# Splitting a head pair's value product by part: all high parts in the even head's step, all low parts in the odd head's

## The chip, the cores and the metric

The kernel runs on one core of a Trainium2 chip. The metric is the time of one execution on the device in microseconds (us). Engines are called PE (TensorE; PEld is its weight load), DVE (VectorE), ACT (ScalarE), POOL (GpSimd) and SP (SyncE). A wait is written "consumer <- producer".

## The reference

One layer of a hybrid backbone: an input projection, retention heads and attention heads side by side, an output projection, expert-choice experts and a final norm, for 2048 latent tokens and 128 context tokens. The change touches attention only, which for each block of 128 queries and each of 8 heads of width 64 computes

```
s = einsum('bkgqd,bskd->bkgqs', qblk, k) * scale     # 16 key tiles of latents and one of context
p = softmax(s, axis=-1)
o = einsum('bkgqs,bskd->bkgqd', p, v)
```

Latent queries read 17 key tiles (2176 keys), context queries only the context tile.

## The kernel before

Every fp32 product is made of high and low parts held as fp32r: a high part is a rounded copy (ACT), a low part what is left of the value (DVE subtracts). The stages follow one another with a barrier between them: conditioning, projection, retention, attention, output projection, selection, experts, final norm.

Attention goes over query tiles i = 0 to 15 (latent) and NT = 16 (context), and in each over heads h = 0 to 7. One pass for one head is called a step here. Tiles 2 to 14 are one loop body, the others are written out. Each engine has its own order of a step's events, a list written by hand: PE_STEP (L999), ACT_STEP (L1001), DVE_STEP (L1003). PE's is: turn 0, turn 1, value 0, value 1, turn 2, turn 3, scores 0, value 2, scores 2, turn 4, fold (even steps; modulation in steps 5 and 7), scores 1.

- `turn` n (L1264): transposes four key tiles of the head's probabilities (turn 4: one) into one of two PSUM banks `a_ps_t`, used alternately. It waits until the bank was emptied. ACT copies the bank into `a_pT_hi` (L1405), DVE subtracts that into `a_pT_lo` (L1507) and so empties the bank.
- `scores` n (L1246): scores of head h+2 for banks 0 and 1 (scores 0), 2 and 3 (scores 1) or 4 (scores 2). It waits until ACT's exponential has read the old scores (`exped`). DVE takes the maxima (L1480), which for scores 1 are the last and lead to the negated maximum `a_nm` (L1490).
- `value` (L1273): the values of a head pair (group) against its turned probabilities, summed in `a_ps_o`. The pair 2g, 2g+1 is taken in steps 2g+2 and 2g+3, in six pieces (PIECES, L1006), three in the even step and three in the odd one. For each key tile the high and the low matmul stand behind one another. The stationary operand is the values' tile (both parts side by side, 128 columns), the moving one the pair's 256 columns. Before the first piece PE waits for both banks to be emptied (the low parts of the step before) and for `o_kept` (ACT has copied the sums of the group before).
- `fold` (L1294) adds the halves of a finished group; DVE's `combine` (L1547) divides by the softmax sum. After step 3 the attention output of the tile before is turned (`out`, L1313), before step 6 the next tile's queries (`q`, L1234).

The context tile has only turn 4 and scores 2 in a step, but the first two of its steps still take the value pieces of tile 15's last pair; its own pairs are one key tile wide.

Of the kernel before, what the change touches and what calls it, by code (L numbers as in the profile page):

```python
# [15 lines left out]
NQ = 8  # L16
NKV = 2
QPK = NQ // NKV
# [973 lines left out]
KEY_TILES = NT + 1  # L992
# [3 lines left out]
CTX_KEYS = NT + 1  # L996
# [6 lines left out]
DVE_STEP = [("turn", 0), ("turn", 1), ("total", 0), ("turn", 2), ("turn", 3), ("scores", 0), ("turn", 4), ("scores", 2),  # L1003
            ("fold", 0), ("scores", 1)]
SEG_ORDER = [0, 2, 1]
PIECES = [(0, 3), (3, 6), (6, 9), (9, 12), (12, 15), (15, KEY_TILES)]  # L1006
GROUP = 2
NGRP = NQ // GROUP

# [1 line left out]
def attention(nc, g, a, s):  # L1011


    with ExitStack() as ctx:
# [4 lines left out]
        vals = k.sb("a_vals", [P, NK, NKV, 2, HD], F32R)  # L1019
# [7 lines left out]
        pT_hi = [k.sb(f"a_pT_hi{i}", [P, KEY_TILES, GROUP, P], F32R) for i in range(2)]  # L1027
        pT_lo = [k.sb(f"a_pT_lo{i}", [P, KEY_TILES, GROUP, P], F32R) for i in range(2)]
# [11 lines left out]
        ps_o = k.ps("a_ps_o", [P, GROUP, P])  # L1040
# [6 lines left out]
        sum_ok, rsum_ok, hi_kept = k.sem("a_sum_ok"), k.sem("a_rsum_ok"), k.sem("a_hi_kept")  # L1047
        filled, emptied = k.sems("a_filled", 2), k.sems("a_emptied", 2)
        fold_ok, valued, o_kept = k.sem("a_fold_ok"), k.sem("a_valued"), k.sem("a_o_kept")
# [95 lines left out]
        def group_index(i, n):  # L1145

            return i * NGRP + n
# [67 lines left out]
        def _(pe):  # L1215
# [57 lines left out]
            def value(t, grp, piece, uses_before):  # L1273

                ctx_tile = isinstance(t, int) and t == NT
                if piece == 0:
                    for b in range(2):
                        pe.wait_ge(emptied[b], uses_before[b])
                    if not (isinstance(t, int) and t == 0 and grp == 0):
                        pe.wait_ge(o_kept, group_index(t, grp))  # L1280
                lo, hi = PIECES[piece]
                kts = range(lo, hi) if not ctx_tile else ([KEY_TILES - 1] if piece == 0 else [])
                for c in kts:
                    src = CTX_KEYS if ctx_tile else c
                    for part in (pT_hi, pT_lo):
                        first = piece == 0 and c == kts[0] and part is pT_hi
                        last = part is pT_lo and c == KEY_TILES - 1
                        ins = nc.tensor.matmul(ps_o[:, :, :],  # L1288
                                               vals[:, src, grp * GROUP // QPK, :, :].rearrange("p d f -> p (d f)"),
                                               part[grp % 2][:, c, :, :], start=first, stop=last)  # L1290
                if kts and kts[-1] == KEY_TILES - 1:
                    ins.then_inc(valued, 1)

            def fold_halves(t, grp, bank):  # L1294
# [30 lines left out]
            start = Bank(-1)  # L1325
# [6 lines left out]
            def body(i):  # L1332
                bank = Bank(i)
                for h in range(NQ):
                    uses_before = [bank.uses_of(b) for b in range(2)]
                    for kind, n in step_events(i, h):
                        if kind == "q":
                            turn_queries(i + 1, n, bank)
                            q_uses = [bank.uses_of(b) for b in range(2)]
                        elif kind == "scores":  # L1340
                            scores(*score_of(i, h), n, q_uses if h >= NQ - 2 else None)
                        elif kind == "turn":
                            turn(i, h, n, bank)
                        elif kind == "value":
                            value(*group_of(i, h), h % 2 * 3 + n, uses_before)
                        elif kind == "fold":
                            fold_halves(*fold_of(i, h), bank)
                        elif kind == "mod":
                            modulation(i, n, bank)
                        else:  # L1350
                            turn_out(i - 1, n, bank)
                if isinstance(i, int) and i == NT:
                    uses_before = [bank.uses_of(b) for b in range(2)]
                    fold_halves(i, NGRP - 2, bank)
                    value(i, NGRP - 1, 0, uses_before)
                    fold_halves(i, NGRP - 1, bank)
                    for half_at in range(2):
                        turn_out(i, half_at, bank)
# [1248 lines left out]
```

## Time and profile before

| | |
|---|---|
| median of 3 runs | 3443.71 us (3442.35 to 3448.79) |
| profiled execution | 3446.82 us, of which the profile's span is 3445.1 us |
| PE busy | 3122.0 us (91%), PEld 2855.8 us (83%) |
| DVE, ACT, POOL busy | 1872.4 (54%), 1716.9 (50%), 396.7 us (12%) |
| mean granted TensorE clock | 0.951 |
| attention, 1000 to 1300 us: busy PE, DVE, ACT; clock | 291.15, 246.08, 224.46 us; 1.00 |
| first value matmul of a step to that of the next, steps 0 to 7, tile from 1205.61 us | 7.09, 6.38, 6.95, 7.58, 6.61, 9.83, 6.57, 7.43 us |
| waits of PEld's scores for ACT's exponential, 820 to 1600 us | 9.4 us, 27 times |
| value matmuls of attention (L1288) | 1092 with high and 1092 with low probabilities |

Where the table names no stretch it is over the whole span. Attention lies between about 690 and 1697 us, its steady part between 820 and 1655. In a timeline a row is a run of like instructions, with start, length, engine, line, operation, operands and count; in brackets stands the engine's idle time before it and what ended that. Matmuls are pipelined, so that the distance of starts, not the length of a row, is what one costs.

### The profile page before, as it was taken

To read this page: it belongs to the slowest core of one execution; us is meant where nothing else is said; L and a number is where in the kernel's file an instruction comes from. 1 tells how busy PE (TensorE), PEld (TensorE's weight loads), DVE (VectorE), ACT (ScalarE), POOL (GpSimd) and SP (SyncE) were. 2 spreads that over 40 slices of the span, in tenths; PEclk is the share of its full clock that TensorE was granted. 3 is DMA by queue.
4 is the path that set the end of the run, shared out by engine and by line. 5 is a ranking of instruction groups with operands and counts; after the bars stand their busy time and mean duration, and the time that the engine had idled before them with its cause. 6 is when DMAs were issued, how large, how long until landed. Compare 5 with 4: busy or idle time off the path is not lost. (4 is left out here: it accounts for less than half of the span.)

```text
span 3445.1 us, 59312 instructions
## 1 busy us (share of the span) xinstructions
PE 3122.0 (91%) x21600; PEld 2855.8 (83%) x21600; DVE 1872.4 (54%) x3255; ACT 1716.9 (50%) x3375; POOL 396.7 (12%) x386
## 2 busy tenths in 40 slices
PE   6899997769999999999699857999999999999991
PEld 6788886658888888888588756999999999999991
DVE  2122224858888888888533383554445555454543
ACT  2222222557777777777433334555554445554542
POOL 0233333500000000000000000111111111111101
PEclk9999998979999999999799857999999999999995
DMA  6112114311000000000244316666666566655546
GB/s 219 49 66 78 62 61 145 129 43 29 19 27 18 22 20 24 21 24 22 73 145 160 118 28 200 196 185 187 185 186 187 178 186 190 186 184 184 184 123 226
DMA packets 315924, 393.74 MB, mean 114 GB/s; under 512 B 30321, under 2 KB 272193, under 8 KB 314817
## 3 DMA queue, kind: packets, MB, share of 16 engines
q1 hardware_dynamic: 302000, 338.64, 30.1%
q0 software_dynamic: 10240, 35.66, 4.6%
q10 hardware_dynamic: 3600, 18.35, 1.3%
q8 instruction: 50, 0.82, 0.1%
q14 instruction: 34, 0.27, 0.0%
HBM read 318.68 MB, written 74.06 MB: 114 GB/s over the span
## 5 line engine op out<-in xcount | busy, mean ns | idle before, releaser
L2423 DVE TENSOR_TENSOR e_w_lo<-e_raw,e_w_hi 128x2048 fp32r<-128x2048 f32 x192 | 440.1, 2292 | 490.7 <-ACT e_w_hi L2365 490.7
L93 PE MATMUL e_ps<-e_x_hi,e_w_hi 128*128 128x272 f32 x2048 | 602.2, 294 | 5.5 <-issue 5.5
L95 PE MATMUL e_ps<-e_x_hi,e_w_lo 128*128 128x272 f32 x2048 | 593.9, 290 | 0.0
L94 PE MATMUL e_ps<-e_x_lo,e_w_hi 128*128 128x272 f32 x2048 | 590.3, 288 | 0.0
L1507 DVE TENSOR_TENSOR a_pT_lo<-a_ps_t,a_pT_hi 128x512 fp32r<-128x512 f32 (+1 forms) x648 | 368.3, 601 | 137.2 <-ACT a_pT_hi L1405 136.9
L1405 ACT ACTIVATE a_pT_hi<-a_ps_t 128x512 fp32r<-128x512 f32 (+1 forms) x648 | 319.6, 532 | 171.0 <-PE a_ps_t L1270 166.2
L93 PEld LDWEIGHTS e_ps<-e_x_hi,e_w_hi 128*128 128x128 f32 x2048 | 386.3, 189 | 7.1 <-issue 5.5
L94 PEld LDWEIGHTS e_ps<-e_x_lo,e_w_hi 128*128 128x128 f32 x2048 | 387.1, 189 | 0.0
L95 PEld LDWEIGHTS e_ps<-e_x_hi,e_w_lo 128*128 128x128 f32 x2048 | 386.1, 189 | 0.0
L2365 ACT ACTIVATE e_w_hi<-e_raw 128x2048 fp32r<-128x2048 f32 x192 | 366.1, 1907 | 14.6 <-DMA e_raw<-in_w_gate 10.2
L1480 DVE TENSOR_REDUCE a_mx<-a_ps_s 128x1 f32<-128x896 f32 (+2 forms) x392 | 346.7, 892 | 26.7 <-PE a_ps_s L1260 26.7
L1270 PE MATMUL a_ps_t<-ident,a_prob 128*128 128x128 f32 x2184 | 329.8, 280 | 27.3 <-DVE a_pT_lo L1507 17.1
L1260 PE MATMUL a_ps_s<-a_keys,a_qT 128*128 128x448 f32 (+2 forms) x1296 | 342.3, 379 | 8.6 <-ACT a_prob L1397 6.5
L1397 ACT ACTIVATE a_prob<-a_ps_s,a_nm 128x896 f32<-128x896 f32 (+2 forms) x392 | 334.9, 859 | 19.0 <-DVE a_nm L1490 16.6
L1270 PEld LDWEIGHTS a_ps_t<-ident,a_prob 128*128 128x128 f32 x2184 | 245.0, 141 | 81.1 <-DVE a_pT_lo L1507 49.0
L93 PE MATMUL e_ps<-e_h_hi,e_w_hi 128*128 128x272 f32 x1024 | 298.2, 291 | 0.0
L95 PE MATMUL e_ps<-e_h_hi,e_w_lo 128*128 128x272 f32 x1024 | 296.3, 289 | 0.0
L94 PE MATMUL e_ps<-e_h_lo,e_w_hi 128*128 128x272 f32 x1024 | 294.8, 288 | 0.0
L1288 PE MATMUL a_ps_o<-a_pT_hi,a_vals 128*128 128x256 f32 x1092 | 282.8, 292 | 2.6 <-DVE a_pT_lo L1507 1.5
L1288 PE MATMUL a_ps_o<-a_pT_lo,a_vals 128*128 128x256 f32 x1092 | 271.7, 282 | 0.0
L93 PE MATMUL p_psP<-w_in_hi,p_hhi 128*128 128x512 f32 (+1 forms) x680 | 254.3, 374 | 4.7 <-DVE p_hlo L415 4.7
L95 PE MATMUL p_psP<-w_in_hi,p_hlo 128*128 128x512 f32 (+1 forms) x680 | 255.6, 376 | 0.0
(284 smaller groups left out, 5430.7 us busy)
## 6 DMA issues: line engine op xcount, KB each, us to landing
e_raw<-in_w_gate SPq DMA_DIRECT2D x64, 1024.0 KB, 5.1
e_raw<-in_w_up SPq DMA_DIRECT2D x64, 1024.0 KB, 5.2
e_raw<-in_w_down SPq DMA_DIRECT2D x64, 1024.0 KB, 5.1
s_ret<-p_pr SPq DMA_DIRECT2D x17, 768.0 KB, 3.6
m_raw<-in_w_in ACTq DMA_DIRECT2D x8, 1152.0 KB, 7.7
o_cT<-s_ct SPq DMA_DIRECT2D x17, 512.0 KB, 5.0
s_x<-o_x SPq DMA_DIRECT2D x17, 512.0 KB, 5.0
s_xn<-o_xn SPq DMA_DIRECT2D x17, 512.0 KB, 3.7
```

What stands on the lines that cost most here:

```text
L93: nc.tensor.matmul(out, w_hi, x_hi, start=first, stop=False)
L94: nc.tensor.matmul(out, w_hi, x_lo, start=False, stop=False)
L95: return nc.tensor.matmul(out, w_lo, x_hi, start=False, stop=last)
L1260: ins = nc.tensor.matmul(ps_s[:, b, 0:w], qT[:, h, :], keys[:, part, h // QPK, src:src + w], start=(part == 0), stop=(part == 1))
L1270: ins = nc.tensor.transpose(ps_t[b][:, c % 4, :], prob[h % 2][:, c * P:(c + 1) * P], g["ident"][:, :])
L1288: ins = nc.tensor.matmul(ps_o[:, :, :], vals[:, src, grp * GROUP // QPK, :, :].rearrange("p d f -> p (d f)"), part[grp % 2][:, c, :, :], s ...
L1397: nc.scalar.activation(seg_probs(i, h, seg), seg_scores(seg, seg_width(i, seg)), ACT.Exp, bias=nm[:, h % 2:h % 2 + 1], scale=scale, accum_ ...
L1405: nc.scalar.activation(out, ps_t[b][:, 0:out.shape[1], :], ACT.Copy).then_inc(hi_kept, 1)
L1480: nc.vector.tensor_reduce(mx[:, h % 2, seg:seg + 1], seg_scores(seg, seg_width(i, seg)), AXY, ALU.max)\
L1507: nc.vector.tensor_tensor(pT_lo[h // 2 % 2][:, out, h % 2, :], ps_t[b][:, 0:m, :], pT_hi[h // 2 % 2][:, out, h % 2, :].bitcast(F32), ALU.s ...
L2365: nc.scalar.activation(w_hi[n % RING][:, :, :], raw[n % RING][:, :, :], ACT.Copy).then_inc(w_hi_ok, 1)
L2423: nc.vector.tensor_tensor(w_lo[n % RING][:, :, :], raw[n % RING][:, :, :], w_hi[n % RING][:, :, :].bitcast(F32), ALU.subtract).then_inc(w_ ...
```

## The change

The pieces become (0, 6), (6, 11), (11, 17), and the even step takes all of them with the high parts, the odd step all again with the low parts. The wait for the emptied banks moves from the even step's first piece to the odd step's; the even step's first piece waits for the pair's last high copy (`hi_kept`) instead. The context tile's own groups keep one high and one low matmul in piece 0 and both waits, and wait for the banks in the odd step too, ahead of an empty piece. The sum of `a_ps_o` is of the same products in another order.

```diff
-PIECES = [(0, 3), (3, 6), (6, 9), (9, 12), (12, 15), (15, KEY_TILES)]
+PIECES = [(0, 6), (6, 11), (11, KEY_TILES)]
@@ value(t, grp, piece, uses_before)
-                if piece == 0:
+                low, n = divmod(piece, len(PIECES))
+                if n == 0 and (low or ctx_tile):
                     for b in range(2):
                         pe.wait_ge(emptied[b], uses_before[b])
+                if piece == 0:
+                    if not ctx_tile:
+                        pe.wait_ge(hi_kept, (t * NQ + GROUP * (grp + 1)) * 5)
                     if not (isinstance(t, int) and t == 0 and grp == 0):
                         pe.wait_ge(o_kept, group_index(t, grp))
-                lo, hi = PIECES[piece]
-                kts = range(lo, hi) if not ctx_tile else ([KEY_TILES - 1] if piece == 0 else [])
-                for c in kts:
-                    src = CTX_KEYS if ctx_tile else c
-                    for part in (pT_hi, pT_lo):
-                        first = piece == 0 and c == kts[0] and part is pT_hi
-                        last = part is pT_lo and c == KEY_TILES - 1
-                        ins = nc.tensor.matmul(ps_o[:, :, :],
-                                               vals[:, src, grp * GROUP // QPK, :, :].rearrange("p d f -> p (d f)"),
-                                               part[grp % 2][:, c, :, :], start=first, stop=last)
-                if kts and kts[-1] == KEY_TILES - 1:
+
+                def product(c, src, part, first, last):
+                    return nc.tensor.matmul(ps_o[:, :, :], vals[:, src, grp * GROUP // QPK, :, :].rearrange("p d f -> p (d f)"),
+                                            part[grp % 2][:, c, :, :], start=bool(first), stop=bool(last))
+
+                if ctx_tile:
+                    if piece == 0:
+                        product(KEY_TILES - 1, CTX_KEYS, pT_hi, True, False)
+                        product(KEY_TILES - 1, CTX_KEYS, pT_lo, False, True).then_inc(valued, 1)
+                    return
+                for c in range(*PIECES[n]):
+                    ins = product(c, c, pT_lo if low else pT_hi, not low and c == 0, low and c == KEY_TILES - 1)
+                if piece == 2 * len(PIECES) - 1:
                     ins.then_inc(valued, 1)
```

## Rows read from the trace of the kernel before

**Rows 1.** Waits from 820 to 1600 us: total us, times, longest

```profile
PEld a_ps_t L1270 <- DVE a_pT_lo L1507: 38.2, 131, 0.7
```

**Rows 2.** Instructions on the tile a_ps_o: ns min/median/max; engine idle before them

```profile
L1288 PEld LDWEIGHTS a_ps_o<-a_pT_hi,a_vals x1092: 186/188/333, 753.9 to 1691.7; 128*128 128x128 f32 x182
...
  DVE a_pT_lo L1507: 3.4, 4
```

**Rows 3.** Timeline of PEld, end of step 7 to step 1: turns, first value loads

```profile
1204.62 1.00 PEld L1270 LDWEIGHTS a_ps_t<-ident,a_prob 128*128 128x128 f32 x8
1205.59 0.19 PEld L1288 LDWEIGHTS a_ps_o<-a_pT_hi,a_vals 128*128 128x128 f32 x1
...
1211.71 1.00 PEld L1270 LDWEIGHTS a_ps_t<-ident,a_prob 128*128 128x128 f32 x8
1212.68 0.19 PEld L1288 LDWEIGHTS a_ps_o<-a_pT_hi,a_vals 128*128 128x128 f32 x1
```

**Rows 4.** Timeline, step 0: three value matmuls in sequence

```profile
1206.77 0.28 PE L1288 MATMUL a_ps_o<-a_pT_lo,a_vals 128*128 128x256 f32 x1
...
1206.89 0.28 PE L1288 MATMUL a_ps_o<-a_pT_hi,a_vals 128*128 128x256 f32 x1
...
1207.01 0.28 PE L1288 MATMUL a_ps_o<-a_pT_lo,a_vals 128*128 128x256 f32 x1
```

**Rows 5.** Timeline, step 0: low parts of turns 0 and 1; turns 2, 3

```profile
1206.82 1.29 DVE L1507 TENSOR_TENSOR a_pT_lo<-a_ps_t,a_pT_hi 128x512 fp32r<-128x512 f32 x2 [0.33 <-ACT a_pT_hi L1405]
...
1207.57 0.42 PEld L1270 LDWEIGHTS a_ps_t<-ident,a_prob 128*128 128x128 f32 x4 [0.48 <-DVE a_pT_lo L1507]
...
1208.16 0.42 PEld L1270 LDWEIGHTS a_ps_t<-ident,a_prob 128*128 128x128 f32 x4 [0.17 <-DVE a_pT_lo L1507]
```

**Rows 6.** Timeline, steps 4 and 6: the same instructions

```profile
1234.08 1.29 DVE L1507 TENSOR_TENSOR a_pT_lo<-a_ps_t,a_pT_hi 128x512 fp32r<-128x512 f32 x2 [0.60 <-ACT a_pT_hi L1405]
...
1235.01 0.90 PEld L1270 LDWEIGHTS a_ps_t<-ident,a_prob 128*128 128x128 f32 x8
...
1250.47 1.29 DVE L1507 TENSOR_TENSOR a_pT_lo<-a_ps_t,a_pT_hi 128x512 fp32r<-128x512 f32 x2 [0.94 <-ACT a_pT_hi L1405]
...
1251.46 0.90 PEld L1270 LDWEIGHTS a_ps_t<-ident,a_prob 128*128 128x128 f32 x8
```

**Rows 7.** Timeline, steps 1 and 3: exponential, turn 4 and scores 1

```profile
1216.20 1.03 ACT L1397 ACTIVATE a_prob<-a_ps_s,a_nm 128x896 f32<-128x896 f32 x1
...
1217.02 0.27 PE L1270 MATMUL a_ps_t<-ident,a_prob 128*128 128x128 f32 x1
1217.37 1.08 PE L1260 MATMUL a_ps_s<-a_keys,a_qT 128*128 128x448 f32 x4
...
1230.38 0.27 PE L1270 MATMUL a_ps_t<-ident,a_prob 128*128 128x128 f32 x1
1230.65 1.08 PE L1260 MATMUL a_ps_s<-a_keys,a_qT 128*128 128x448 f32 x4
```

**Rows 8.** Timeline, steps 5 and 7: turn 4, modulation, and what follows

```profile
1245.15 0.27 PE L1270 MATMUL a_ps_t<-ident,a_prob 128*128 128x128 f32 x1
1245.26 1.85 PE L1309 MATMUL a_ps_t<-cc,a_wm 128*128 128x2 f32 x16
...
1248.50 1.09 ACT L1408 ACTIVATE a_qT<-a_ps_t 128x512 fp32r<-128x512 f32 x2 [2.76 <-PE a_ps_t L1241]
...
1261.08 0.27 PE L1270 MATMUL a_ps_t<-ident,a_prob 128*128 128x128 f32 x1
1261.35 1.06 PE L1309 MATMUL a_ps_t<-cc,a_wm 128*64 128x2 f32 x16
```

**Rows 9.** Timeline, context tile, steps 0 and 1

```profile
1670.29 0.36 PE L1288 MATMUL a_ps_o<-a_pT_hi,a_vals 128*128 128x256 f32 x1 [0.29 <-issue]
...
1674.12 0.28 DVE L1550 TENSOR_TENSOR a_att<-a_ps_t,a_rsum 128x128 f32<-128x128 f32 x1
...
1675.18 0.34 PE L1260 MATMUL a_ps_s<-a_keys,a_qT 128*128 128x128 f32 x2
```

## The prediction

> **What bounds the kernel now.** I first read the busy shares by slice of the page: in attention PE is busy nearly throughout, DVE and ACT well over half. The table by stretch says the same of 300 steady us (in the table above): PE 291 us, DVE 246, ACT 224, the clock at its full level, 1.00. So PE sets the time, unless it waits. The list of waits says for whom: 131 times in 780 us PE's next transposes wait for DVE's low parts, 38.2 us in all [rows 1], and 27 times, two in a tile, the scores wait for ACT's exponential (9.4 us). The timeline of one tile then shows where in a step. The tile between 1205 and 1264 us (58.4 us, the sum of the step lengths in the table above) stands for 16; its step lengths return in the tiles of the loop within 0.05 us.
>
> In a step the wait is at turns 2 and 3, behind pieces 0 and 1. Turn 2 needs the bank of turn 0, which DVE frees with its first low part, turn 3 that of turn 1. In step 0 the two low parts run from 1206.82 to 1208.11; turn 2 starts at 1207.57, turn 3 at 1208.16, each right behind its own [rows 5]. Steps 1, 2, 3, 5 and 7 look the same (a wait of about 0.18 us before turn 3 in each). The low parts in turn hang on scores 1 of the step before, over the last maxima. So in six steps of eight the time goes round a ring: scores 1, maxima, low parts, turn 3, and then PE's own work up to the next scores 1. Pieces 0 and 1 lie beside the ring. Piece 2 lies on it.
>
> **The waits that are moved.** The wait taken from the even step is empty before the change. Turns 0 and 1 stand ahead of it on PE and have waited for the same two banks. The trace agrees: DVE ends idle time before a value matmul 4 times in all, 3.4 us, mostly in the context tile [rows 2]. The waits' own price: from the first load of turns 0 and 1 to the first value load it is 0.97 us in step 0 (three waits) and 0.97 us in step 1 (none) [rows 3]. So one wait fewer in the even step and two more in the odd one are priced at 0. What is queued behind them on PE are the value matmuls; who waits for those is ACT's copy of the sums, a step later. Bounds: a gain of 3.4 us, and a loss of 0.01 us in each of 64 odd steps, under 1 us.
>
> **Order of the matmuls.** 34 matmuls per pair before and after. Neighbours start 0.12 us apart, from low to high (other weights) as from high to low (same weights) [rows 4]. So giving up the neighbours with equal weights costs 0. Every matmul has a load of its own even now; the 1092 high ones have 1092 loads [rows 2]. The Trainium skill, "TensorE: Matmul & The Clock Gate", section "Step-by-step: what each phase is for", speaks against the change here: weights should be loaded once and used by several matmuls. By this rule the old order would have saved a load per pair and the new one lose it; the trace does not agree, as both transitions take 0.12 us.
>
> **Where the matmuls go.** Pieces were 6, 6, 6 matmuls in the even and 6, 6, 4 in the odd step; they become 6, 5, 6 in both. So pieces 0 and 1 shrink from 12 to 11 everywhere, piece 2 stays 6 in even steps and grows from 4 to 6 in odd ones.
>
> Pieces 0 and 1: PE comes 0.12 us earlier to turn 2. In the six steps of the ring it waits that much longer: 0. In steps 4 and 6 PE is the later one. In step 4 the low parts end at 1234.08 + 1.29 = 1235.37; turn 2 loads from 1235.01, turn 3 four loads of some 0.11 us later, at 1235.46 [rows 6]. With 0.05 us from DVE's end to PE's start (1208.11 to 1208.16 in step 0, [rows 5]) turn 3 can't start before 1235.42, so 0.04 us is gained. In step 6: low parts until 1251.76, turn 3 at 1251.91 [rows 6], gain 0.10 us. Together 0.14 x 16 tiles = 2.2 us gained. Bounds: 0 and 0.24 x 16 = 3.8 us.
>
> Piece 2, odd steps: 2 x 0.12 = 0.24 us more between turn 3 and scores 1, by step:
> - Step 5: turn 4 at 1245.15, the modulation right behind at 1245.26, then scores 1 and the queries' transposes, for which ACT has waited 2.76 us [rows 8]. Nothing covers it: +0.24.
> - Step 1: scores 1 starts at 1217.37, 0.35 us after turn 4, where a transpose takes 0.11; it waits for the exponential that runs from 1216.20 to 1217.23 [rows 7], which itself hangs on turn 3. Cover 0.24 us, all of it used: 0. If that cover is gone, +0.24.
> - Step 3: scores 1 comes 0.27 us after turn 4 [rows 7], cover 0.16. Scores 1 is 0.08 late, but the transposes of the output behind it wait for DVE (turn 4's low part): 0. Without that, +0.08 to +0.24.
> - Step 7: the modulation comes 0.27 us after turn 4 [rows 8]; it waits for DVE's low part of turn 3. Cover 0.16 by the starts of the matmuls, and more if their loads can run ahead: +0.00 to +0.08, I take 0.04. In tile 15 turn 4 waits for DVE anyway: 0.
>
> Sum: 16 x 0.24 + 15 x 0.04 = 3.8 + 0.6 = 4.4 us lost. Bounds: 0, were there cover in step 5 too, and 64 x 0.24 = 15.4 us, were there none at all.
>
> **The context tile.** Step 0 takes 17 matmuls instead of 18 (0.12 us), and its first no longer waits for DVE's copy of the modulation; it had idled 0.29 us there [rows 9]. So 0.4 us early. Step 1 now waits, ahead of the low parts, for the banks of step 0, the last of which is freed by DVE's division, 1674.12 + 0.28 = 1674.40 [rows 9]; before, the 16 matmuls followed the fold at once. They start at 1674.0 (0.4 early), take 17 x 0.12 + 0.08 = 2.1, and scores 2 follows at 1676.1 to 1676.2 instead of 1675.18 [rows 9]: +1.0 us, on a chain of latencies, so all of it. In steps 3, 5 and 7 the empty piece waits for the banks too, with scores 2 (turn 4 in step 7) queued behind it; the scores there wait longer for ACT. 0, with a bound of 1 us for the three.
>
> **Sum.** -2.2 + 4.4 + 1.0 = +3.2 us, on the profiled execution's 3446.82 us (1.7 us outside its span): 3450.0. That execution is 3.1 us above the median of the three runs; on the median, 3443.71 + 3.2 = 3446.9 us.
>
> **The rivals.** (A) As summed, +1 to +6 us. Chance 0.62.
> (B) Neutral: PE's work is the same and what one piece loses the other gets back; step 5 has cover, or steps 4 and 6 give their full 0.24. -3 to +1 us, 3441 to 3445. For it: nothing is added. Against it: the ring [rows 5] and ACT's 2.76 us [rows 8]. Chance 0.14.
> (C) Faster: the lifted wait is real where the profile doesn't show it. That gives at most 3.4 us [rows 2], with the full 3.8 us in steps 4 and 6 and all of piece 2 covered: -7.2 us, 3436.5. The change doing nothing of what it says (the wait is met anyway) is part of A and B. Chance 0.06.
> (D) Slower: the ring takes all of piece 2's growth in every odd step, because the cover in steps 1, 3 and 7 moves along with the delay. 15.4 - 2.2 + 1.0 = +14.2 us, 3457.9. It decides from about half of that cover on. For it: the cover in step 1 is exactly used up. Against it: the exponential hangs on turn 3, which isn't moved. Chance 0.17.
> (E) Reloading weights costs after all: a load of 0.19 us against a spacing of 0.12 [rows 2, 4] leaves 0.07 us bare in some 1088 low matmuls, 76 us, 3520. The equal spacings say no. Chance 0.01.
>
> **How the numbers follow.** About 0.2% (6.9 us) is what a measurement of this kernel tells from no change. A and B lie within it: same 0.76. C is faster, 0.06. D and E are slower, 0.18. The range reaches from B and the lower part of the runs' own scatter, 3440, to D's 3458; C and E stay outside.
>
> **What would show it.** In the trace after: 17 matmuls in each step's pieces; turns 2 and 3 of steps 0, 1, 2, 3, 5, 7 behind DVE's low parts as before, with the wait 0.12 us longer; the time from step 5's first value matmul to step 6's up from 9.83 to 10.07 us, from step 1's to step 2's unchanged at 6.38; the wait for the exponential gone in step 1; the first low matmul of the context tile's step 1 behind DVE's division. It is wrong if the steps 1 and 3 grow, if steps 0 or 2 change, or if matmuls with changing weights stand more than 0.12 us apart.

## The result and the profile after

The changed kernel takes 3453.06 us in the median of 20 runs (3447.52 to 3455.16), the kernel before 3444.42 us (20 runs, 3441.68 to 3448.89). The ratio is 1.0023, with a 95% interval of 1.0017 to 1.0030: slower by 5.9 to 10.3 us. The forecast was +3.2 us. The time lies inside the stated range, but the likeliest case, A, was too small, and the outcome fell on the side that had been given 0.18. Ratios are taken over the undisturbed executions: among the 15 of the kernel before that stand beside e5 to e8, one took 10325.14 us at a granted clock of 0.294 and is left out.

Two lines of the page of the changed kernel, its span and the busy times of PE, PEld, DVE, ACT and POOL:

```profile
span 3449.9 us, 59378 instructions
PE 3119.0 (90%) x21600; PEld 2853.3 (83%) x21600; DVE 1872.6 (54%) x3255; ACT 1716.5 (50%) x3375; POOL 396.9 (12%) x386
```

The engines work no longer than before (PE 3122.0, DVE 1872.4, ACT 1716.9 us) and run the same number of matmuls. What was lost is waiting. Two rows of the waits from 820 to 1600 us (total us, times, longest):

```profile
PEld a_ps_t L1270 <- DVE a_pT_lo L1513: 51.4, 159, 0.9
PE a_ps_t L1270 <- DVE a_pT_lo L1513: 19.7, 51, 0.7
```

The wait of the transposes' weight loads for the low parts went from 38.2 us in 131 waits [rows 1] to 51.4 in 159, as had been expected of pieces 0 and 1, which are one matmul shorter. The 28 new waits, two in a tile, stand before turn 2 of steps 1 and 3, where the list had shown none. In the matmuls' own row it went from 12.9 us in 39 waits to 19.7 in 51. The wait of PE's scores for ACT's exponential (9.4 us, 27 times before) is no longer in the list.

The distances between the first value matmuls of neighbouring steps tell where the time went. A typical tile of the loop, in us; equal steps agree from tile to tile and from run to run within about 0.03 us. e6 and e9, left out here, have the step lengths of e2 and of the changed kernel. "12/6" means 12 value matmuls ahead of turn 2 and 6 behind turn 3:

| kernel | even, odd steps | 0 | 1 | 2 | 3 | 4 | 5 | 6 | 7 | tile |
|---|---|---|---|---|---|---|---|---|---|---|
| before | 12/6, 12/4 | 7.09 | 6.38 | 6.95 | 7.57 | 6.62 | 9.83 | 6.57 | 7.43 | 58.44 |
| after | 11/6, 11/6 | 7.08 | 6.37 | 6.96 | 7.57 | 6.61 | 10.05 | 6.56 | 7.63 | 58.83 |
| e1, old order | 11/6, 11/6 | 7.07 | 6.37 | 6.96 | 7.57 | 6.62 | 10.05 | 6.57 | 7.62 | 58.83 |
| e2 | 11/6, 13/4 | 7.07 | 6.38 | 6.96 | 7.57 | 6.61 | 9.83 | 6.56 | 7.44 | 58.42 |
| e3 | 13/4, 13/4 | 6.90 | 6.40 | 6.96 | 7.57 | 6.62 | 9.84 | 6.57 | 7.44 | 58.30 |
| e4 | 11/6, 9/8 | 7.07 | 6.51 | 6.88 | 7.69 | 6.62 | 10.31 | 6.56 | 7.86 | 59.50 |
| e5 | 9/8, 13/4 | 7.32 | 6.38 | 7.20 | 7.54 | 6.62 | 9.83 | 6.57 | 7.45 | 58.91 |
| e7, old order | 13/6, 13/2 | 7.09 | 6.38 | 6.96 | 7.57 | 6.62 | 9.85 | 6.57 | 7.44 | 58.48 |
| e8, old order | 13/4, 11/6 in steps 0, 1 | 6.89 | 6.41 | 6.96 | 7.57 | 6.62 | 9.83 | 6.57 | 7.44 | 58.29 |

After the change only steps 5 and 7 differ, by 0.22 and 0.19 to 0.20 us. From the first value matmul of attention to the modulation of tile 15's step 7 it is 915.06 us before (753.88 to 1668.94) and 921.16 after (754.74 to 1675.90): 6.1 us. From there to the last transposes of attention it is 25.74 us (to 1694.68) and 26.96 (to 1702.86): 1.2 us. So attention carries 7.3 us, inside the interval of the runs. The spans of the two profiled executions differ by 4.8 us only. Outside attention they scatter: the one after begins attention 0.9 us later and makes up 3.4 us behind it, in stages that the change doesn't touch.

Step 5 after the change, answering to [rows 8]:

```profile
1249.48 0.27 PE L1270 MATMUL a_ps_t<-ident,a_prob 128*128 128x128 f32 x1
1249.58 1.85 PE L1315 MATMUL a_ps_t<-cc,a_wm 128*128 128x2 f32 x16
1251.29 1.05 PE L1260 MATMUL a_ps_s<-a_keys,a_qT 128*128 128x448 f32 x4
```

The modulation again starts 0.10 us behind turn 4: nothing lies between, and everything after it is late by the two matmuls. Step 7, with the low parts of turns 2 and 3:

```profile
1264.22 1.29 DVE L1513 TENSOR_TENSOR a_pT_lo<-a_ps_t,a_pT_hi 128x512 fp32r<-128x512 f32 x2 [0.77 <-ACT a_pT_hi L1411]
...
1265.62 0.27 PE L1270 MATMUL a_ps_t<-ident,a_prob 128*128 128x128 f32 x1
...
1265.82 1.09 PE L1315 MATMUL a_ps_t<-cc,a_wm 128*64 128x2 f32 x16
```

Here turn 4 and modulation are 0.20 us apart, although the low part of turn 3 had ended at 1265.51. Before they were 0.27 apart [rows 8]. So the cover had been at most 0.07 us, not 0.16. From turn 4 to scores 1 it is 1.27 us before (1261.08 to 1262.35) and 1.22 after (1265.62 to 1266.84), which leaves 0.24 - 0.05 = 0.19 us of growth, as measured.

### The profile page after: what moved, and what is told of

It reads as the page before. It is cut to its first block and busy times, and to the rows that moved or that the text cites. A ratio compares the mean times of both kernels' runs of the same rounds, so it can differ in the third digit from the quotient of the medians.

```text
span 3449.9 us, 59378 instructions
## 1 busy us (share of the span) xinstructions
PE 3119.0 (90%) x21600; PEld 2853.3 (83%) x21600; DVE 1872.6 (54%) x3255; ACT 1716.5 (50%) x3375; POOL 396.9 (12%) x386
## 5 line engine op out<-in xcount | busy, mean ns | idle before, releaser
L2371 ACT ACTIVATE e_w_hi<-e_raw 128x2048 fp32r<-128x2048 f32 x192 | 366.1, 1907 | 14.7 <-DMA e_raw<-in_w_gate 10.3
L94 PE MATMUL p_psP<-w_in_lo,p_hhi 128*128 128x512 f32 (+1 forms) x680 | 253.8, 373 | 0.0
L1260 PEld LDWEIGHTS a_ps_s<-a_keys,a_qT 128*128 128x128 f32 x1296 | 219.1, 192 | 20.2 <-ACT a_prob L1403 5.3
```

What stands on the lines that cost most here:

```text
L94: nc.tensor.matmul(out, w_hi, x_lo, start=False, stop=False)
L1260: ins = nc.tensor.matmul(ps_s[:, b, 0:w], qT[:, h, :], keys[:, part, h // QPK, src:src + w], start=(part == 0), stop=(part == 1))
L2371: nc.scalar.activation(w_hi[n % RING][:, :, :], raw[n % RING][:, :, :], ACT.Copy).then_inc(w_hi_ok, 1)
```

## Experiments

**e1: the new sizes in the old order.** The kernel before, with only this (and the loop over single matmuls that it needs):

```diff
-PIECES = [(0, 3), (3, 6), (6, 9), (9, 12), (12, 15), (15, KEY_TILES)]
+PIECES = [(0, 6), (6, 11), (11, 17), (17, 23), (23, 28), (28, 2 * KEY_TILES)]
...
+                for m in range(lo, hi):
+                    c, part = m // 2, (pT_hi, pT_lo)[m % 2]
```

> The old order (high and low matmul of a key tile behind one another) and the old waits, but the pieces hold 6, 5, 6 matmuls in both steps, as in the changed kernel. Theory R (the sizes alone: two more matmuls in the odd step's piece 2, which stands between turn 3 and scores 1): step 5 at 10.05 us and step 7 at 7.63 us as in the changed kernel, the other steps as before, the context tile as before; about +6 us on the time before, ratio 1.0015 to 1.002. Rival O (the new order of the matmuls or the moved waits cost the time): steps 5 and 7 at 9.83 and 7.44 us, ratio 1.000.

Measured: 3452.68 us against 3445.58, ratio 1.0020 (1.0011 to 1.0029), and the step lengths are those of the changed kernel, within 0.02 us. High beside low with equal weights, or 17 high ones in a row with changing weights, with the waits in the old or the new place: no step tells them apart. Rival O fell, and the title of the change describes the part of it that costs nothing. That the context tile stayed as before could not be read off here, since the clock was low in part of it:

```profile
1676.32:1679.61 3.29, 3.29 (x17) 3.29 (x18) 0.15 (x1) 0.00 (x0) 0.00 (x0) 0.59 0.02 5
```

This is the stretch view (time, then busy PE, PEld, DVE, ACT, POOL, granted clock, DMA share, GB/s) of the first value matmuls of that tile; the clock averages 0.59. Behind it the loss of the changed kernel is absent: from the fold to the last transposes of attention it is 22.04 us in e1 (1680.16 to 1702.20), 21.85 before (1672.83 to 1694.68) and 23.52 after the change (1679.34 to 1702.86).

**e2: the odd step's piece 2 back at 4.** The changed kernel with

```diff
+LOW_PIECES = [(0, 7), (7, 13), (13, KEY_TILES)]
-                for c in range(*PIECES[n]):
+                for c in range(*(LOW_PIECES if low else PIECES)[n]):
```

> The changed kernel with the low pieces cut 7, 6, 4 instead of 6, 5, 6, so that the odd step's piece 2 has its old 4 matmuls and pieces 0 and 1 together 13; the high pieces stay 6, 5, 6. Theory R: steps 5 and 7 back at 9.83 and 7.44 us, steps 1 and 3 unchanged (turn 2 comes up to 0.1 us later there, turn 3 had waited 0.18 us), so only the context tile's 1.2 us are left: ratio 1.000 to 1.0005. Rival O: nothing comes back, ratio 1.002. Rival S (PE's work in a step counts, wherever it stands): as the odd step still has 17 matmuls instead of 16 and the even one 17 instead of 18, the ratio of the changed kernel stays.

Measured: 3445.61 us against 3445.58, ratio 1.0001 (0.9992 to 1.0010). Steps 5 and 7 are back at 9.83 and 7.44 us with the order, the waits and the 17 matmuls per step of the changed kernel. So it is neither the order nor the amount of work in a step (rival S), but what stands behind turn 3 in the odd steps.

**e4: the odd step's piece 2 at 8.** Low pieces (0, 5), (5, 9), (9, KEY_TILES).

> The changed kernel with the low pieces cut 5, 4, 8: two more matmuls behind turn 3 in odd steps than in the changed kernel. Theory R: the cover by ACT's exponential in steps 1 and 3 (0.24 and 0.16 us) was used up by the first two, so now all four odd steps of a tile grow by 0.24 us over the changed kernel: 0.96 us per tile, 15 us in all, ratio to the time before 1.006 to 1.0075. If steps 1 and 3 have cover beyond that: ratio about 1.0045. Rival O: ratio 1.002.

Measured: 3462.29 us against 3445.58, ratio 1.0046 (1.0032 to 1.0060): the second of the three cases. Steps 5 and 7 grow by 0.26 and 0.23 us over the changed kernel, again the whole of two matmuls. Step 1 grows by 0.14 and step 3 by 0.12, and step 2 gets 0.08 back. The cover in steps 1 and 3 was larger than read. Turn 4 and scores 1 of these two steps in e4:

```profile
1227.21 0.27 PE L1271 MATMUL a_ps_t<-ident,a_prob 128*128 128x128 f32 x1
1227.23 1.06 PE L1261 MATMUL a_ps_s<-a_keys,a_qT 128*128 128x448 f32 x4
...
1240.62 0.27 PE L1271 MATMUL a_ps_t<-ident,a_prob 128*128 128x128 f32 x1
1240.65 1.05 PE L1261 MATMUL a_ps_s<-a_keys,a_qT 128*128 128x448 f32 x4
```

With nothing to wait for, scores 1 starts 0.02 and 0.03 us behind turn 4, not 0.11. Before the change it was 0.35 and 0.27 [rows 7], so the cover was 0.33 and 0.24 us. In step 1 that leaves 0.48 - 0.33 = 0.15 of four matmuls, as measured. In step 3 half of the remaining 0.24 was taken elsewhere; the prediction named the output's transposes, which no run isolates.

**e3: 13 and 4 everywhere.** PIECES = [(0, 7), (7, 13), (13, KEY_TILES)] for both parts.

> The changed kernel with all pieces cut 7, 6, 4: 13 matmuls ahead of turn 2 and 4 behind turn 3 in both steps. Theory R: even steps have 2 matmuls fewer on the ring. Steps 0 and 2 lose 0.24 us each, for turns 2 and 3 had waited longer there than the one added matmul takes; steps 4 and 6 between 0 and 0.24 us each, as they are held by ACT's chain or by PE; odd steps as before the change. Per tile -0.5 to -0.95 us, in all -7 to -14 us on the time before with the context tile's +1.2: ratio 0.996 to 0.998. Rivals O and S: ratio 1.000 to 1.002, since the same matmuls stand in the same order as in the changed kernel.

Measured: 3446.31 us against 3445.58, ratio 1.0001 (0.9992 to 1.0010). A miss of theory R. Two matmuls fewer behind turn 3 brought 0.17 us in step 0 and nothing in steps 2, 4 and 6. The ring alone doesn't tell the length of an even step; something else is level with it. That led to theory C, tested from both sides by e5 and e7.

**e5: the even step's piece 2 at 8.** High pieces (0, 5), (5, 9), (9, KEY_TILES), low pieces as in e2.

> High pieces 5, 4, 8, low pieces 7, 6, 4: the even step has 9 matmuls ahead of turn 2 and 8 behind turn 3, the odd step 13 and 4. Taking two away from the even step's piece 2 had changed nothing in steps 2, 4 and 6 and 0.17 us in step 0. Theory C (two chains run from turn 3 to scores 1 side by side: PE's own work, and ACT's copy and DVE's low part of turn 3, for whose bank the fold waits; with 6 matmuls in piece 2 they are nearly level): two matmuls more lie bare but for a small remainder, steps 0, 2, 4 and 6 grow by 0.15 to 0.24 us each, 0.6 to 0.9 us per tile. Rival X (steps 2, 4 and 6 are held by ACT's or DVE's work altogether, PE has room): they stay at 6.96, 6.62 and 6.57 us, only step 0 grows.

Measured (one execution, 3449.93 us): against e2, steps 0 and 2 grow by 0.25 and 0.24 us, steps 4 and 6 stay at 6.62 and 6.57. Theory C held in steps 0 and 2 and rival X in steps 4 and 6, which keep their length whether 4, 6 or 8 matmuls stand behind turn 3 (with 13, 11 or 9 ahead of turn 2). ACT's timeline of step 6, in the changed kernel, shows why:

```profile
1252.81 1.09 ACT L1414 ACTIVATE a_qT<-a_ps_t 128x512 fp32r<-128x512 f32 x2 [2.75 <-PE a_ps_t L1241]
1253.78 0.39 ACT L1423 ACTIVATE a_o_sum<-a_ps_o 128x256 f32<-128x256 f32 x1
1254.15 1.09 ACT L1411 ACTIVATE a_pT_hi<-a_ps_t 128x512 fp32r<-128x512 f32 x2
1255.13 1.00 ACT L1403 ACTIVATE a_prob<-a_ps_s,a_nm 128x896 f32<-128x896 f32 x1
...
1256.67 1.09 ACT L1411 ACTIVATE a_pT_hi<-a_ps_t 128x512 fp32r<-128x512 f32 x2
1257.62 1.04 ACT L1403 ACTIVATE a_prob<-a_ps_s,a_nm 128x896 f32<-128x896 f32 x1
```

ACT comes in late, with the queries' copies, and then works without a gap to the exponential of 1257.62. Turns 2 and 3 may come earlier on PE, their high copies don't start before 1256.67. DVE's low parts follow these copies, and the fold, which needs the bank of turn 3, follows the low parts:

```profile
1257.31 1.29 DVE L1513 TENSOR_TENSOR a_pT_lo<-a_ps_t,a_pT_hi 128x512 fp32r<-128x512 f32 x2 [0.97 <-ACT a_pT_hi L1411]
...
1258.71 0.52 PEld L1306 LDWEIGHTS a_ps_t<-a_fold,a_o_sum 128*128 128x128 f32 x4 [0.24 <-issue]
```

The low parts end at 1258.60, and the fold's load starts 0.11 us later. In step 4 ACT comes in late with the copies of the output and has no wait from the high copy of 1237.54 to the exponential of 1241.00 either. In e5 the copy of turn 4 behind that exponential was the one to wait for PE, by 0.30 us, and that was still caught up:

```profile
1257.61 0.28 ACT L1412 ACTIVATE a_pT_hi<-a_ps_t 128x128 fp32r<-128x128 f32 x1 [0.30 <-PE a_ps_t L1271]
```

That ACT's chain sets steps 4 and 6 is read from these rows and from the flat lengths; a kernel in which ACT had less to do there was not run, so the cause there is argued and not shown.

**e7: the odd step's piece 2 at 2.** Old order and waits:

```diff
+PIECES = [(0, 7), (7, 13), (13, 19), (19, 26), (26, 32), (32, 2 * KEY_TILES)]
```

> Old order and old waits, pieces of 7, 6, 6 matmuls in the even and 7, 6, 2 in the odd step: two matmuls less than before the change behind turn 3 in odd steps. Theory R as it stood in the prediction (in step 5 piece 2 lies bare, whatever its size): step 5 falls from 9.83 to 9.60 us. Theory C (the modulation there waits for the bank of turn 3, whose low part ends 0.12 us before it starts; PE's work and that chain were level with 4 matmuls): step 5 stays at 9.80 to 9.83, step 7 at 7.44, and nothing is gained in odd steps. Even steps have 13 matmuls ahead of turn 2: steps 0 and 2 unchanged, steps 4 and 6 up to 0.1 us longer.

Measured (one execution, 3447.60 us): step 5 at 9.85, step 7 at 7.44. Nothing is gained: theory C. Step 5 in its trace:

```profile
1244.52 1.29 DVE L1505 TENSOR_TENSOR a_pT_lo<-a_ps_t,a_pT_hi 128x512 fp32r<-128x512 f32 x2 [0.52 <-ACT a_pT_hi L1403]
1245.51 0.14 PEld L1270 LDWEIGHTS a_ps_t<-ident,a_prob 128*128 128x128 f32 x1
1245.68 0.27 PE L1270 MATMUL a_ps_t<-ident,a_prob 128*128 128x128 f32 x1
1245.93 1.86 PEld L1307 LDWEIGHTS a_ps_t<-cc,a_wm 128*128 128x128 f32 x16 [0.28 <-issue]
```

Turn 4 is early, but the modulation needs the bank of turn 3, and DVE's low part there ends at 1244.52 + 1.29 = 1245.81. The load follows at 1245.93, 0.42 us behind that of turn 4. So in step 5 two chains from turn 3 were level with 4 matmuls; more lie bare at full price, fewer bring nothing. The same kernel tells of the cover of steps 1 and 3. Its scores wait for the exponential (list of waits from 820 to 1600 us; us in all, times, longest):

```profile
PEld a_ps_s L1260 <- ACT a_prob L1395: 15.7, 27, 0.6
```

Before it was 9.4 us in 27 waits, 0.35 us in each and 0.23 us less than here, which is the two matmuls. After the change there is none in the list.

**e6 and e9: the context tile.** The odd step waits for the banks as they stood when the even step began, which is enough for the pair's last low part. e6 is e2 with this, e9 the changed kernel with this:

```diff
-                        pe.wait_ge(emptied[b], uses_before[b])
+                        pe.wait_ge(emptied[b], (even_uses if low else uses_before)[b])
                 if piece == 0:
+                    even_uses[:] = uses_before
```

> The kernel with high pieces 6, 5, 6 and low pieces 7, 6, 4 once more, but the odd step's low pieces wait for the banks as they stood at the start of the even step, which covers the pair's last low part, and not for what the even step itself put in. Tiles 0 to 15 unchanged. Context tile: if the wait for DVE's division was the cause of its loss, the first low matmul of its step 1 stands right behind the fold again (its distance from the first high matmul falls from 4.14 us by about 1.2 us to 2.9), and from there to the end all is 1.1 to 1.2 us earlier. If not, the distance stays.

> The changed kernel as it is (pieces 6, 5, 6 twice), but the odd step's low pieces wait for the banks as they stood at the start of the even step. Steps as in the changed kernel: 10.05 us for step 5, 7.63 us for step 7. Context tile, if the wait for DVE's division is the whole cause of its loss: from step 0's fold to the scores of step 1 2.5 us instead of 3.8 us, 1.3 us less, and the low matmuls without a wait ahead of them. If the loss comes from anything else in that tile (the order of the matmuls, the empty pieces), the distance stays at 3.8 us. The time as a whole moves by 1.3 us, which one execution can't tell.

The changed kernel's context tile, steps 0 and 1 (fold, DVE's division, low matmuls, scores of step 1), answering to [rows 9]:

```profile
1679.34 0.56 PE L1306 MATMUL a_ps_t<-a_fold,a_o_sum 128*128 128x64 f32 x4
...
1680.63 0.28 DVE L1556 TENSOR_TENSOR a_att<-a_ps_t,a_rsum 128x128 f32<-128x128 f32 x1
...
1681.06 2.27 PE L1287 MATMUL a_ps_o<-a_pT_lo,a_vals 128*128 128x256 f32 x17 [1.16 <-DVE a_att L1556]
...
1683.16 0.34 PE L1260 MATMUL a_ps_s<-a_keys,a_qT 128*128 128x128 f32 x2
```

And in e9:

```profile
1679.61 0.56 PE L1309 MATMUL a_ps_t<-a_fold,a_o_sum 128*128 128x64 f32 x4
1679.97 2.27 PE L1290 MATMUL a_ps_o<-a_pT_lo,a_vals 128*128 128x256 f32 x17
1682.08 0.34 PE L1260 MATMUL a_ps_s<-a_keys,a_qT 128*128 128x128 f32 x2
```

The wait of 1.16 us is gone and fold to scores takes 2.47 instead of 3.82 us, with the steps as in the changed kernel. To the last transposes of attention it is 22.24 us (1679.61 to 1701.85) instead of 23.52 (1679.34 to 1702.86). From the modulation to those transposes e9 takes 25.69 us (1676.16 to 1701.85), against 25.74 before and 26.96 after the change, at granted clocks of 0.70, 0.71 and 0.73: the wait for a bank that nobody needed was this tile's whole loss. In e6 the low matmuls also follow the fold at once (1674.60 and 1674.96), but the distance from its first high matmul didn't fall to 2.9 us, it was 4.31. The high matmuls themselves ran at a low clock there, which took 1.52 us (see below). In e9, where their clock was 1.00, the distance is 2.81 us (1677.16 to 1679.97). The times of these two, 3448.09 and 3453.50 us, are single executions and tell nothing of 1.3 us.

**e8: only where it paid.** The kernel before, whose last pair alone is cut 7, 6, 4 and 6, 5, 6 (old order, old waits):

```diff
+LAST_PIECES = [(0, 7), (7, 13), (13, 17), (17, 23), (23, 28), (28, 2 * KEY_TILES)]
...
+                lo, hi = (LAST_PIECES if grp == NGRP - 1 else PIECES)[piece]
```

> The kernel before, in which only the last pair (steps 0 and 1 of the next tile) is cut 7, 6, 4 and 6, 5, 6, in the old order with the old waits. Step 0 has its two matmuls less behind turn 3 (it had gained 0.17 us by that), step 1 two more (it had taken them under ACT's exponential for nothing). By theories R and C alike step 0 at 6.90 us, the rest as before: 0.17 us in each of 14 or 15 tiles, 2.5 us, ratio 0.9990 to 0.9995, about the size that can just be told. If the cover in step 1 depends on what step 0 does, step 1 grows and nothing is gained.

Measured: 3443.59 us against 3446.14, ratio 0.9993 (0.9984 to 1.0002). Step 0 lost its 0.18 to 0.20 us, step 1 took 0.03 of it back, a tile is 0.15 us shorter. The interval contains 1, so it isn't shown that the kernel as a whole is faster.

## Why the prediction was right and wrong

- **The moved waits, at 0 in tiles 0 to 15: right.** Steps 0 to 3 are unchanged, and e1, with the old waits, has all its steps at the lengths of the changed kernel. The idle time before value loads that DVE's low parts end was not won back: 3.4 us in 4 waits before, 4.6 in 5 after. The fifth is the context tile's, and e9 is at 3.4 in 4 again.
- **The order of the matmuls, at 0: right.** By e1 against the changed kernel. Neighbours with equal weights save nothing here: the 1092 high and 1092 low matmuls have 1092 loads each, after the change too.
- **Pieces 0 and 1 in the six steps of the ring, at 0: right.** The wait for the low parts grew instead.
- **Pieces 0 and 1 in steps 4 and 6, at -2.2 us: wrong.** They are at 6.61 and 6.56 us, as before. The step that failed is "in steps 4 and 6 PE is the later one": PE was later than DVE's low parts, but turns 2 and 3 feed ACT, and ACT was later than both. I had followed what ends the wait in front of turn 2, and not asked whether what turn 2 releases was in a hurry.
- **Piece 2, step 5, at +0.24: right**, 0.22 us measured, 3.5 us over 16 tiles. That nothing covers it held only upward: e7 shows a second chain just below.
- **Step 7, at +0.04: mis-sized.** 0.19 to 0.20 us measured, 2.9 us over 15 tiles. Cover was read as the distance of modulation and turn 4 less the 0.11 us that step 5 shows. With no low part to wait for, the two are 0.20 us apart in this step (the changed kernel, and e4 too), so the natural distance was taken from the wrong row. Why it is 0.20 here and 0.10 in step 5 stays open; the row names no engine.
- **Steps 1 and 3, at 0: right.** Their lengths didn't move, and the wait for the exponential is gone. The fear of D, that the cover moves along, fell. The cover was mis-read all the same: 0.33 and 0.24 us by e4, where the prediction had 0.24 and 0.16, since it took 0.11 us for the natural distance of turn 4 and scores 1.
- **The context tile, at +1.0: right in mechanism and nearly in size**, 1.2 us. Of these 1.02 lie between the modulation and the scores of step 1 (6.24 us before, 7.26 after). The wait for DVE's division is seen in the trace and taken away in e9.

The sum by what was measured is 3.5 + 2.9 + 1.2 = 7.6 us, against 7.3 in the trace and 5.9 to 10.3 in the runs. Of the 4.4 us between this and the forecast, steps 4 and 6 are 2.2 and step 7 is 2.3. Both errors had the same sign: a gain counted that wasn't there, a cover counted that wasn't. The chances followed the sum, and 0.76 for no difference was too much for a sum of four terms, three of them resting on tenths of a microsecond of cover.

## What to carry to other kernels

A step written out by hand can have several chains that are level: here PE's own work, ACT's copies and DVE's low parts all run from turn 3 to the next maxima. Work moved onto any of them costs its full price at once, and work taken off brings nothing until the next chain is shorter too, so price a move in both directions separately, and look at who waits for the earlier result before counting a gain. A cover read as "distance less the natural distance" needs the natural distance of the same instruction in the same place: from turn 4 to what follows it on PE it was 0.02, 0.03, 0.10 and 0.20 us in steps 1, 3, 5 and 7. And a wait that is moved should name the use that it protects, not the latest one: a count taken a step later waited 1.16 us for a bank that had nothing to do with it.

## What was unexpected of the hardware

The clock fell while TensorE was busy. In e6 the 17 value matmuls of the context tile's step 0, up to its scores, take 3.65 us, in e2 2.13. The stretch views, first e6, then e2 (granted clock in the third column from the end):

```profile
1670.65:1674.30 3.65, 3.65 (x20) 3.65 (x19) 0.37 (x3) 0.35 (x2) 0.00 (x0) 0.53 0.02 4
```

```profile
1671.19:1673.32 2.13, 2.13 (x19) 2.13 (x18) 0.38 (x3) 0.35 (x2) 0.00 (x0) 1.00 0.00 0
```

A granted clock of 0.53 is nearly all 1.2 GHz, 1.00 is 2.4 GHz. In both runs the modulation just before them, 1 us of busy PE, was granted 1.00. Ahead of it PE had waited twice, by 0.33 and 0.36 us, in e6 and in e2 alike, and e6 has the same order of work up to that point. What made the difference stays open. The low clock cost 1.5 us in e6 and about 1.2 us in e1 (3.29 us against 2.13), as much as the wait under study. A distance in a tile like this one can be compared only together with the clock of its stretch.
